# Four slots of split weights instead of three, the second context's transposes in the first feed-forward, and whole square sums in the state-space output

## What is computed

```python
def first_block(x, c, ctx, c_ctx, ...):
    for i in range(DEPTH):
        ...
        ul = snake(modulate(hl, m_l[0], m_l[1]))
        uc = modulate(hc, m_c[0], m_c[1])
        ...
        hl = layer_norm(DEEPNORM_ALPHA * hl + m_l[2] * snake(yl), ln_g[i, 0], ln_b[i, 0])
        hl = layer_norm(DEEPNORM_ALPHA * hl + m_l[5] * sq_relu_mlp(modulate(hl, m_l[3], m_l[4]), ffn_w1[i], ffn_w2[i]),
                        ln_g[i, 1], ln_b[i, 1])
        ...

def ssd_mixer(uc, ul, w_in, ..., norm_g, w_out, need_ctx):
        ...
        return rms_norm(y * jax.nn.silu(z), norm_g) @ w_out, (s_f, s_b)

def second_block(x, c, ctx, c_ctx, ...):
    for l in range(DEPTH):
        ...
        h = rms_norm_2(x, norm_g[l]) * (1.0 + scale[:, None]) + shift[:, None]
        hc = rms_norm_2(ctx, norm_g[l]) * (1.0 + scale_c) + shift_c
        ...
        x_new = x + gate[:, None] * merge_branches(o_na, o_mla, o_diff, z, gm, w_br[l], w_out[l])
        ...
```

## Time and profile before

| | before |
|---|---|
| median of 3 runs | 2761.93 us (2757.51 to 2763.64) |
| profiled execution, its own time | 2756.06 us |
| its span | 2753.9 us |
| mean granted clock of PE | 0.946 |
| PE busy | 2504.5 us, 91% |
| DVE busy | 1376.1 us, 50% |
| ACT busy | 1190.3 us, 43% |
| POOL busy | 639.9 us, 23% |
| split weights: ACT's roundings | 398 of 1.05 us |
| subtractions on POOL, on DVE | 158 of 2.44 us, 240 of 1.25 us |

### The profile page before, as it was taken

The page is one execution under the profiler, slowest core; times in us unless marked ns, Lnnn a source line. Parts: engine busy times, 40 slices in busy tenths (PEclk is TensorE's granted clock), DMA queues, the critical chain, the costliest instruction groups (busy, mean ns, idle before and its releaser), DMA issues. The chain is left out here.

```text
span 2753.9 us, 34978 instructions
## 1 busy us (share of the span) xinstructions
PE 2504.5 (91%) x13700; PEld 1980.5 (72%) x13700; DVE 1376.1 (50%) x2126; ACT 1190.3 (43%) x1995; POOL 639.9 (23%) x394
## 2 busy tenths in 40 slices
PE   6996878999998998998997999899999979989988
PEld 3783447888878887578996767577767757758777
DVE  2206667433444666336665534543565344454665
ACT  1823324422326432444554345554365233555362
POOL 1437640000005343110001432002301116403310
PEclk8999998999998999978998999899999999999999
DMA  6326842333324332744663231222222213334333
GB/s 230 84 84 214 288 145 71 99 98 93 91 84 131 92 85 62 252 131 130 193 197 100 69 85 50 65 54 67 77 62 69 84 54 105 98 88 112 85 100 107
DMA packets 414874, 302.11 MB, mean 110 GB/s; under 512 B 10290, under 2 KB 386712, under 8 KB 414712
## 3 DMA queue, kind: packets, MB, share of 16 engines
q1 hardware_dynamic: 413600, 299.45, 36.9%
q10 hardware_dynamic: 1112, 0.44, 0.1%
HBM read 298.80 MB, written 1.05 MB: 109 GB/s over the span
## 5 line engine op out<-in xcount | busy, mean ns | idle before, releaser
L207 POOL TENSOR_TENSOR weights_lo<-wslots,weights_hi 128x1024 fp32r<-128x1024 f32 x158 | 384.3, 2438 | 928.2 <-ACT weights_hi L197 369.1
L197 ACT ACTIVATE weights_hi<-wslots 128x1024 fp32r<-128x1024 f32 x398 | 418.9, 1054 | 330.3 <-PE psum L260 295.9
L260 PE MATMUL psum<-input_hi,weights_hi 128*128 128x512 f32 (+1 forms) x1448 | 522.9, 361 | 40.8 <-POOL weights_lo L207 22.6
L260 PE MATMUL psum<-input_hi,weights_lo 128*128 128x512 f32 (+1 forms) x1448 | 509.6, 352 | 0.0
L260 PE MATMUL psum<-input_lo,weights_hi 128*128 128x512 f32 (+1 forms) x1448 | 508.7, 351 | 0.0
L207 DVE TENSOR_TENSOR weights_lo<-wslots,weights_hi 128x1024 fp32r<-128x1024 f32 x240 | 298.0, 1250 | 218.0 <-ACT weights_hi L197 206.6
L260 PEld LDWEIGHTS psum<-input_hi,weights_hi 128*128 128x128 f32 x1448 | 278.4, 192 | 85.5 <-POOL weights_lo L207 26.2
L260 PEld LDWEIGHTS psum<-input_lo,weights_hi 128*128 128x128 f32 x1448 | 278.5, 192 | 40.1 <-issue 2.9
L260 PEld LDWEIGHTS psum<-input_hi,weights_lo 128*128 128x128 f32 x1448 | 277.9, 192 | 40.1
L260 PE MATMUL psum<-ffn_hidden_hi,weights_hi 128*128 128x512 f32 (+1 forms) x512 | 172.2, 336 | 2.0 <-issue 2.0
L260 PE MATMUL psum<-ffn_hidden_hi,weights_lo 128*128 128x512 f32 (+1 forms) x512 | 171.4, 335 | 0.0
(11 more groups left out here) (421 smaller groups left out, 4885.4 us busy)
## 6 DMA issues: line engine op xcount, KB each, us to landing
wslots<-w_in SPq DMA_DIRECT2D x132, 512.0 KB, 3.9
wslots<-ffn_w SPq DMA_DIRECT2D x128, 512.0 KB, 4.1
wslots<-ada_w SPq DMA_DIRECT2D x96, 512.0 KB, 4.8
wslots<-ssd_w_in SPq DMA_DIRECT2D x49, 512.0 KB, 3.9
wslots<-w_ada SPq DMA_DIRECT2D x48, 512.0 KB, 4.5
wslots<-gla_w_in SPq DMA_DIRECT2D x25, 512.0 KB, 3.8
wslots<-w_br SPq DMA_DIRECT2D x24, 512.0 KB, 3.9
wslots<-ssd_w_out SPq DMA_DIRECT2D x16, 512.0 KB, 4.5
```

What stands on the lines that cost most here:

```text
L197: act.activation(self.part(self.whi_r, n), self.slot(n), ACT.Copy)\
L207: engine.tensor_tensor(self.part(self.wlo_r, n), self.slot(n), self.part(self.whi, n), ALU.subtract)\
L260: ins = pe.matmul(out_of(self.bank(g)), l, r, start=first and i == 0, stop=last and i == len(pairs) - 1, skip_group_check=not (first and l ...
```

## The change

- `RING` goes from 3 to 4 and `AHEAD` from 2 to 3: four slots of high and low parts, filled three ahead.
- The memory for it comes from laying buffers over others: the squares and accumulators of `LayerSums`, the gains of a layer norm, the latent attention's `mla_x` and `mla_sq`, the neighbourhood attention's bias tiles. For the first branch of the mixing (r = 0) the sigmoids' ring has 3 places (one of its own, two in the output's buffer) in place of 4, and ACT waits for the product that many tiles back.
- The second context's tokens: two transfers of 512 KB ahead of the feed-forward's weight stream in the first layer, transposes on PE behind tiles 3 to 10 of the first `up`, copies on ACT one tile later.
- `ssd_out`: the squares are summed with the 128 x 128 ones as stationary operand and 256 columns of squares moving, so that each partition holds each token's sum. The spreading on PE and its copy on ACT are gone, and the root and the reciprocal are of 128 x 256.

```diff
@@ -48,12 +48,12 @@
 RAW = 4
-RING = 3
+RING = 4
 SLOT = 1024
...
 FIRST = 3
-AHEAD = 2
+AHEAD = 3
 MIX_BANKS = (1, 2, 3)
@@ -710,12 +710,12 @@
-    def __init__(self, b, st, l, gate, seg, g0, late, rate=None):
+    def __init__(self, b, st, l, gate, seg, g0, late, rate=None, sq=None, acc=None):
         self.b, self.l, self.gate, self.seg, self.g0, self.late = b, l, gate, seg, g0, late
...
         self.shift = b.sb(st, "ln_shift", [P, self.n])
-        self.sq = b.sb(st, "ln_sq", [P, self.RING, self.n])
-        self.acc = b.sb(st, "ln_acc", [P, 2, self.n])
+        self.sq = b.sb(st, "ln_sq", [P, self.RING, self.n]) if sq is None else sq
+        self.acc = b.sb(st, "ln_acc", [P, 2, self.n]) if acc is None else acc[:, :, 0:self.n]
         self.rate = None if rate is None else (rate[:], b.sb(st, "ln_scaled", [P, T]))
@@ -933,8 +934,10 @@
         hid_lo_r, hid_hi_r = hid_lo[:].bitcast(F32R), hid_hi[:].bitcast(F32R)
+        second = l == 0
+        tok = b.H2[:, :, NCTX:T].rearrange("p k (t f) -> p t k f", t=2)
         u0, _, t0, _ = b.phases[f"ffn{l}_up0"]
-        sums = LayerSums(b, st, l, 5, seg, b.phases[f"ffn{l}_down1"][2], 2)
+        sums = LayerSums(b, st, l, 5, seg, b.phases[f"ffn{l}_down1"][2], 2, sq=hid, acc=b.raw)
         layer_norm_stage(b, l, 0, seg, b.H1, (l, 1, u0, t0, [seg] * FIRST))
@@ -942,15 +945,30 @@
             def _(sp):
+                if second:
+                    for t in range(2):
+                        sp.dma_start(tok[:, t], b.dram["ctx_2"][0][t * P:(t + 1) * P].rearrange("p (k f) -> p k f", f=P))\
+                            .then_inc(b.tick("tokens_in", 16), 16)
                 for i in range(2):
...
             def _(pe):
+                def turn_tokens(k):
+                    if k == 0:
+                        pe.wait_ge(b.sem("tokens_in"), b.nth("tokens_in", 32))
+                    if k >= 4:
+                        pe.wait_ge(b.sem("tile_copied"), b.nth("tile_copied", k - 3))
+                    for t in range(2):
+                        ins = pe.transpose(b.psum[:, 4 + k % 4, t * P:(t + 1) * P], tok[:, t, k], b.ident[:])
+                    ins.then_inc(b.tick("tile_turned"), 1)
+
                 for i in range(2):
...
                         b.products(pe, f"ffn{l}_up{i}", j, seg, b.input(seg))
+                        if second and i == 0 and FIRST <= j < FIRST + KD:
+                            turn_tokens(j - FIRST)
                     s0, count, t0, _ = downs[i]
@@ -981,6 +999,11 @@
                             layer_affine(b, act, l, 0, seg, j // 2)
+                        if second and i == 0 and FIRST < j <= FIRST + KD:
+                            k = j - FIRST - 1
+                            act.wait_ge(b.sem("tile_turned"), b.nth("tile_turned", k + 1))
+                            act.activation(b.H2[:, k, 0:NCTX], b.psum[:, 4 + k % 4, 0:NCTX], ACT.Copy)\
+                                .then_inc(b.tick("tile_copied"), 1)
                     round_hidden(i, HT - 1)
@@ -1042,7 +1065,6 @@
         le = b.sb(st, "gla_le", [P, 2, T])
-        tok = b.sb(st, "tok", [P, 2, D])
         with b.stage() as block:
@@ -1056,7 +1078,6 @@
                 b.stream(sp, "gla_a")
-                sp.dma_start(tok[:], d["ctx_2"][0].rearrange("(t p) n -> p t n", p=P)).then_inc(b.tick("tokens_in_2", 16), 16)
                 for phase in ("gla_qk", "gla_v", "gla_g"):
@@ -1088,21 +1109,9 @@
                             logits(n)
-                def turn_tokens(k):
-                    if k == 0:
-                        pe.wait_ge(b.sem("tokens_in_2"), b.nth("tokens_in_2", 16))
-                        pe.wait_ge(b.sem("logit_read"), b.nth("logit_read", 2 * GH))
-                    if k >= 4:
-                        pe.wait_ge(b.sem("tile_copied"), b.nth("tile_copied", k - 3))
-                    for t in range(2):
-                        ins = pe.transpose(b.psum[:, 4 + k % 4, t * P:(t + 1) * P], tok[:, t, k * P:(k + 1) * P], b.ident[:])
-                    ins.then_inc(b.tick("tile_turned"), 1)
...
                     b.products_by_token(pe, "gla_v", s, b.tokens)
-                    if s >= VS:
-                        turn_tokens(2 * (s - VS))
-                        turn_tokens(2 * (s - VS) + 1)
                 for j in range(KD):
@@ -1174,9 +1183,6 @@
                     ins.then_inc(b.tick("gate_summed"), 1)
-                for k in range(KD):
-                    dve.wait_ge(b.sem("tile_turned"), b.nth("tile_turned", k + 1))
-                    dve.tensor_copy(b.H2[:, k, 0:NCTX], b.psum[:, 4 + k % 4, 0:2 * P]).then_inc(b.tick("tile_copied"), 1)
@@ -1489,9 +1495,9 @@
         input_parts(b, st)
-        sq = b.sb(st, "gla_sq", [P, 2, T])
-        rstd = b.sb(st, "gla_rstd", [P, 2, T])
-        sums = LayerSums(b, st, 0, 2, ALL, b.phases["gla_out"][2], FIRST)
+        squares = b.sb(st, "gla_sq", [P, 4, T])
+        sq, rstd = squares[:, 0:2], squares[:, 2:4]
+        sums = LayerSums(b, st, 0, 2, ALL, b.phases["gla_out"][2], FIRST, sq=squares)
         with b.stage() as block:
@@ -1998,22 +2004,22 @@
-def ssd_out(b, xs, z, y):
+def ssd_out(b, xs, z, y, s):
...
         sq = b.sb(st, "ssd_sq", [P, 2, NLAT])
-        stat = b.sb(st, "ssd_stat", [P, 2])
         rate = b.sb(st, "ssd_rate", [P, NLAT])
...
         yh_r, yl_r = yh[:].bitcast(F32R), yl[:].bitcast(F32R)
-        sums = LayerSums(b, st, 1, 2, LAT, b.phases["ssd_out"][2], 2, rate)
+        sums = LayerSums(b, st, 1, 2, LAT, b.phases["ssd_out"][2], 2, rate,
+                         s[:, 0, 0:4 * NLAT].rearrange("p (a t) -> p a t", a=4), s[:, 1, 0:2 * NLAT].rearrange("p (a t) -> p a t", a=2))
         with b.stage() as block:
             w0, _, wt, wn = b.phases["ssd_out"]
-            SUM, SPREAD = 4, 7
+            SUM = 4
@@ -2042,10 +2048,8 @@
                     pe.wait_ge(b.sem("squared"), b.nth("squared", f + 1))
-                    for t in range(2):
-                        ins = pe.matmul(b.psum[:, SUM, t:t + 1], sq[:, f % 2, t * P:(t + 1) * P], b.ones[:, 0:1],
-                                        start=f == 0 and t == 0, stop=f == NF - 1 and t == 1, skip_group_check=True)
-                    ins.then_inc(b.tick("square_added"), 1)
+                    pe.matmul(b.psum[:, SUM, 0:NLAT], b.ones[:], sq[:, f % 2, :], start=f == 0, stop=f == NF - 1,
+                              skip_group_check=True).then_inc(b.tick("square_added"), 1)
@@ -2054,11 +2058,6 @@
                     add_square(f)
-                pe.wait_ge(b.sem("rates_ready"), b.nth("rates_ready", 1))
-                for t in range(2):
-                    ins = pe.matmul(b.psum[:, SPREAD, t * P:(t + 1) * P], stat[:, t:t + 1].broadcast_to([P, P]), b.ident[:],
-                                    start=t == 0, stop=t == 1, skip_group_check=True)
-                ins.then_inc(b.tick("rate_spread"), 1)
                 for s in range(2, 2 * wn):
@@ -2078,11 +2077,9 @@
                 act.wait_ge(b.sem("square_added"), b.nth("square_added", NF))
-                act.activation(stat[:], b.psum[:, SUM, 0:2], ACT.Sqrt, bias=b.eps[:, 1:2], scale=1.0 / SDI)\
+                act.activation(rate[:], b.psum[:, SUM, 0:NLAT], ACT.Sqrt, bias=b.eps[:, 1:2], scale=1.0 / SDI)\
                     .then_inc(b.tick("deviation_ready"), 1)
                 b.round_weights(act, b.last_slot(wt) + AHEAD)
-                act.wait_ge(b.sem("rate_spread"), b.nth("rate_spread", 1))
-                act.activation(rate[:], b.psum[:, SPREAD, 0:NLAT], ACT.Copy).then_inc(b.tick("rate_copied"), 1)
                 for m in range(wn):
@@ -2106,9 +2103,9 @@
                 dve.wait_ge(b.sem("deviation_ready"), b.nth("deviation_ready", 1))
-                dve.reciprocal(stat[:], stat[:]).then_inc(b.tick("rates_ready"), 1)
+                dve.reciprocal(rate[:], rate[:]).then_inc(b.tick("rates_ready"), 1)
                 b.split_weights(dve, "dve", b.last_slot(wt) + AHEAD)
-                dve.wait_ge(b.sem("rate_copied"), b.nth("rate_copied", 1))
+                dve.wait_ge(b.sem("rates_ready"), b.nth("rates_ready", 1))
                 sums.vector(dve)
@@ -2385,8 +2382,9 @@
     with st:
-        x = b.sb(st, "mla_x", [P, 3, MLH, MQK])
-        sq = b.sb(st, "mla_sq", [P, 2, MLH * MQK])
+        room = b.H1[:].rearrange("p k t -> p (k t)")
+        x = room[:, 0:3 * MLH * MQK].rearrange("p (i h c) -> p i h c", i=3, h=MLH)
+        sq = room[:, 3 * MLH * MQK:5 * MLH * MQK].rearrange("p (i n) -> p i n", i=2)
         ss = b.sb(st, "mla_sums", [P, N, MLH])
@@ -2673,8 +2671,7 @@
         if near:
-            biased = b.sb(st, "biased", [P, 2, T])
-            bias = b.sb(st, "bias_tile", [P, 2, T])
+            bias, biased = b.H1[:, 0:2, :], b.H1[:, 2:4, :]
             mask = b.sb(st, "na_mask", [P, NLAT])
@@ -3069,10 +3067,11 @@
         act.wait_ge(b.sem("product_done"), g + 1)
-        if r or p >= 2:
-            back = b.phases[f"mix{l}_{r}"][2] + t - 6 if p >= 2 else b.phases[f"mix{l}_{r - 1}"][2] + 16 + t - 6
```

(7 more changed lines are left out.)

17 lines of the change are left out of this document (10 added, 7 removed).

## The result

The changed kernel took 2714.05 us (median of 4, 2708.95 to 2716.52), the kernel before beside it 2760.14 (4 runs). The ratio is 0.983, with a 95% interval of 0.9811 to 0.9849: faster by 46 us, where 34 had been forecast. The direction and most places were right; the size was not.

A forecast was written before the change was run, and what follows sets the result against it. TensorE was taken as the bound, time being won only where it stands still or runs at its lower clock. Terms summed to -33.4 us: 2722.7 profiled, 2728 median; main range 2719 to 2736, some 8 in 10 within 2714 to 2746.

The forecast's parts named there:

- Where the fourth slot helps: Waits at stage openings go: `ssd_z` -8.5 us, `ssd_xbc` -3.6, second feed-forward -4.2, attention's neighbourhood projections -3.0.
- Elsewhere no wait for weights stands in the trace: 0.: Mix, merge and the second half of each feed-forward: no weight waits to remove, so 0 us.
- The square sums: `ssd_out`: wide sums let PE's clock rise after two feature tiles; loop -8.1, cold products -1.4, end +0.5; -9.0 us.
- The transposes: Second context's transposes move from GLA's projections to the first feed-forward: PE's part 0, token wait +0.4 us.
- The first feed-forward: Opening pause -2.9 and cold stretch -2.7, together -5.6 us; -5.2 in the comparison of terms.
- GLA's term: GLA's first projections: PE's 2.69 us wait and the half-clock stretch behind it both go, -4.4 us.
- Unhidden preparations: Fourth slot's preparation not covered: front +2.3 us, state-space norm +1.2, latent attention's third rounding +2.0 at both layers.
- 1 (clock stays): Clock does not rise in the `ssd_out` loop: total gain only -21.3 us, 2740 us; chance 0.20.
- 2 (late next slot): In `ssd_z`, `ssd_xbc` and attention the pause moves one slot on, 13 of 15.1 us return: 2741 us; chance 0.15.
- 3 (slower): Uncovered preparation before 25 or more of some 30 barriers outweighs the gain: about 2768 us; chance 0.02.
- 5: New loop or tokens stall a queue held for free, leaving time within 0.2% of before; chance 0.03.
- 4 (the phase of the half-clock stretches): Shifted work adds or removes two or three half-clock stretches anywhere: 5 us either way; no chance of its own.

The follow-up runs named there:

- E3: The changed kernel with a ring of four but slots prepared only two ahead (AHEAD 2); 2731.53 us, ratio 0.9898.
- E2: The kernel before with the new square sums of `ssd_out` alone, three slots, two ahead; 2748.26 us, ratio 0.9963.
- E4: The changed kernel, square sums of feature tiles 1 to 15 cut to one column, ones still stationary; 2722.64 us, one run.
- E6: The changed kernel, one single-column matmul per feature tile after the first for the square sum, squares stationary as in the old roles; 2718.09 us.
- E1: The changed kernel with the square sums of `ssd_out` as before; four slots and moved transposes stay; 2730.97 us, ratio 0.9891.
- The repeat: The changed kernel, unaltered, measured again in a second series; 2718.42 us, ratio 0.9843.
- E10: The changed kernel with the fourth slot prepared behind the barrier at the front, layer norms and latent attention; 2715.99 us, ratio 0.9840.

## Why the prediction was right in its direction and wrong in its size

- **Where the fourth slot helps.** Right at three places, within some 2 us: `ssd_z` -9.6 and -10.6 for -8.5, `ssd_xbc` -4.1 and -4.5 for -3.6, the second feed-forward -4.8 for -4.2. E3 confirms the reason for the first two. The terms are all somewhat small, and one cause is that I took the idle time in brackets as the wait's cost. The record before it is longer than the distance to the next matmul (0.39 for 0.23 us, 0.28 for 0.12), and the first matmul behind it is 0.11 longer than the others: 0.27 us for each wait. In the first attention layer I priced the wait of 0.95 us alone; in the trace of before PE's clock is at 0.50 for 6.8 us around it (1530.8 to 1537.6), in that of after for 3.4, and up to the end of these products 2.4 us are gained.
- **"Elsewhere no wait for weights stands in the trace: 0."** This step failed. The earlier trace rows gave 8 waits for DVE, 8.7 us, and I had placed three of them with 7.4 us; the five others stood in `ssd_out` behind the loop, 0.2 to 0.3 us each. With the tails and with those that carry "issue" as their releaser, they cost some 3 us in `ssd_out` and most of the 2.8 in the second feed-forward's last down products. They are some 5.5 of the 13 us that were missing, the largest part that has one cause.
- **The square sums.** The outcome was as forecast (the clock rises early in the loop), the term was somewhat small: E2's stage is 10.3 us shorter for 9.0 (its median 11.3 under before). In the trace of the change the loop gave 9.2 for 8.1, the cold products behind it 1.4 as forecast, and the end gave 0.2 where I had a cost of 0.5 (1.57 us stood between the loop and the next product, now 1.0 and a wait of 0.39); with 3 us of small waits that is the -13.8. But the reason given for the rise, wide columns in the sums, was wrong: E4 and E6 rise without them. That the direction came out all the same is luck as far as this reason goes.
- **The transposes.** "PE's part is the same in both: 0" failed by some 0.6 us: 1.5 saved, 2.6 paid, of which 0.47 is the token wait, forecast as 0.4. The 6.9 us on which that rests were misread as the start-up's: they are the middle of two transfers of 1 MB, 9.1 us in the start-up and 4.8 for `ctx_2` in the GLA layer. After the change the two halves land 4.2 and 5.7 us behind their issue.
- **The first feed-forward.** -2.8 and -1.7 for -5.2. 2.6 us less are the tokens (which I had counted as zero against a zero in GLA's term, and GLA's is -6.6 for -4.4); taken together the two terms are -9.4 and -9.6, as forecast (-9.6). That they meet so closely is luck: the move of the tokens costs 0.7 us more than forecast, and GLA's own part gives about as much more.
- **Unhidden preparations.** Front +2.5, norm +1.0, both forecast; the norm's microsecond is a second DVE subtraction held up, 1.66 us instead of 0.68. The latent attention's third rounding is there in the trace at both layers.
- **Rivals.** 1 (clock stays) did not come. 2 (late next slot) came only as one wait of 0.81 us. 3 (slower) and 5 did not. 4 (the phase of the half-clock stretches) came within its 5 us: counted in windows of 1.7 us, PE's granted clock was lower for 297 us before and 227 after, and of the 56 us of busy time that lay in them less, half is lost time, 28 us. But 15 of it is the `ssd_out` loop, as the earlier trace rows and the stretches of E1 and of the changed kernel show, and 9 are the half-clock stretches behind four waits that the terms had priced (1.7, 2.7, 2.7 and 1.7). That leaves 4 us, with some 1.2 of the neighbourhood projections in it. The repeat has 235 us in place of 227, and the two series differ by 4 us, so some of this is luck.

The range was too narrow on the lower side for a simple reason: nearly every doubt that I had listed made the gain smaller, and the two that make it larger (places not priced, and what a wait costs beside its bracket) were left out.

## What to carry to other kernels

A wait in a trace costs what the distances between the matmuls around it say, not the idle time beside the row; and small waits that repeat once a tile have to be counted by the tile's period before and against the sum of its products. A ring's size and its lead are two things: the size frees the rounding engine in a steady row of tiles, the lead covers the change from one kind of work to the next. Where PE is recorded busy and the clock stays at half, look for stationary operands that are loaded for one column; here taking away half of them was enough. And work that is moved away from a barrier can land beside an engine that it holds up: E10 gained 0.3 of 2.3 us in the front.
